# First expert block's rows gathered by column products from x1 in two tile pairs, with key products and slot table moved behind the first up products

## The reference, cut to what matters

```python
x = x + gt1 * rmsnorm(y, norm_gains[l, 1])
h = rmsnorm(x, norm_gains[l, 2]) * (1.0 + sc2) + sh2
...
group_sel = jnp.argmax(group_logits, axis=-1)
top_p, top_i = lax.top_k(jax.nn.softmax(in_group, axis=-1), TOP_K_IN_GROUP)
expert_ids = group_sel[:, None] * EXPERTS_PER_GROUP + top_i
...
for e in range(N_EXPERTS):
    hid = jax.nn.silu(t @ w_up1[e]) * (t @ w_up3[e])
    y = y + combine[:, e:e + 1] * (hid @ w_down[e])
```

## Time and profile before

| | |
|---|---|
| median of 3 runs | 1086.32 us (1085.09 to 1086.57) |
| profiled execution | 1088.07 us, its span 1086.4 us |
| PE busy | 1023.9 us (94%) |
| DVE busy | 657.9 us (61%) |
| ACT busy | 329.8 us (30%) |
| POOL busy | 135.3 us (12%) |
| moved by DMA | 275.10 MB, 253 GB/s mean |

### The profile page before, as it was taken

One profiled execution on the slowest core, in us unless ns is written; L12 is line 12 of the kernel. 1 busy time (PEld: TensorE's weight loads), 2 busy tenths in 40 slices (PEclk: granted clock), 3 DMA queues, 4 the chain that ended last, 5 costly groups with the idle time before them and its releaser, 6 DMA issues.

```text
span 1086.4 us, 18111 instructions
## 1 busy us (share of the span) xinstructions
PE 1023.9 (94%) x7385; PEld 588.7 (54%) x7385; DVE 657.9 (61%) x1125; ACT 329.8 (30%) x512; POOL 135.3 (12%) x156
## 2 busy tenths in 40 slices
PE   4899999999999999999999999999999999889995
PEld 2578578755556777768884444444433433333342
DVE  2478869364465442248347677777777666566666
ACT  3352462375662324364353110111111110110114
POOL 0100000200000101374401100000000000001003
PEclk9899999999999999999998999999999999999998
DMA  9666403204420004242747999999999999999994
GB/s 343 249 208 216 171 1 137 93 3 162 148 78 2 4 5 157 80 156 98 306 194 310 363 396 401 400 397 403 406 409 407 401 404 392 405 397 400 411 421 194
DMA packets 67733, 275.10 MB, mean 253 GB/s; under 512 B 7742, under 2 KB 17256, under 8 KB 43098
## 3 DMA queue, kind: packets, MB, share of 16 engines
q1 hardware_dynamic: 62976, 263.71, 62.7%
q10 hardware_dynamic: 2218, 6.52, 1.6%
q0 software_dynamic: 2480, 4.01, 1.3%
HBM read 274.13 MB, written 4.21 MB: 256 GB/s over the span
## 4 chain that ended last, share of the span: by engine, by line
PE 50%; SPq 23%; DVE 12%; DMA 7%; ACT 5%; issue 2%; POOL 0%; DVEq 0%; ACTq 0%
SPq L488 16%; PE ps L2231 9%; PE ps L2250 5%; SPq L492 5%; PE ps L1897 3%; DMA arena<-in_w_up 3%; PE ps L2214 2%; SPq L496 2%; PE ps L1878 2%; DMA arena<-in_w_mod 2%; PE ps L1886 2%; PE ps L1995 2%; PE ps L1844 2%; PE ps L1879 1%; PE ps L1880 1%
## 5 line engine op out<-in xcount | busy, mean ns | idle before, releaser
L1558 DVE TENSOR_TENSOR arena<-arena,ps 128x1024 f32<-128x1024 f32 x124 | 145.5, 1215 | 52.6 <-PE ps L2214 52.6
L2231 PE MATMUL ps<-arena 128*64 128x512 f32 x672 | 154.5, 602 | 11.1 <-DMA arena<-in_w_up 10.4
L2231 PEld LDWEIGHTS ps<-arena 128*64 128x64 f32 x672 | 47.8, 138 | 105.0 <-issue 101.3
L1062 ACT ACTIVATE results<-ps,ST 64x512 fp32r<-64x512 f32 x64 | 43.7, 683 | 182.7 <-PE ps L2250 182.2
L1055 ACT ACTIVATE arena<-ps 128x256 f32<-128x256 f32 x32 | 12.3, 384 | 233.9 <-PE ps L2231 233.9
L2250 PE MATMUL ps<-arena 128*64 128x512 f32 x336 | 76.7, 598 | 1.5 <-DMA arena<-in_w_down 1.5
L1735 PE MATMUL ps<-h_upper,w_upper 128*128 128x512 f32 (+1 forms) x184 | 73.9, 402 | 4.4 <-POOL h_lower_first L616 4.2
L2231 PE MATMUL ps<-ring,arena 128*64 128x512 f32 x320 | 72.7, 596 | 4.3 <-DMA ring<-in_w_up 4.3
L1568 DVE SCALAR_TENSOR_TENSOR results<-ps,ST,results 64x512 fp32r<-64x512 f32 x64 | 48.0, 750 | 46.8 <-ACT results L1062 46.3
L2214 PE MATMUL ps<-results,back 128*128 128x512 f32 x248 | 73.8, 419 | 0.0
L1737 PE MATMUL ps<-h_upper,w_lower 128*128 128x512 f32 (+1 forms) x184 | 72.5, 394 | 0.0
(11 more groups left out here) (440 smaller groups left out, 1835.1 us busy)
## 6 DMA issues: line engine op xcount, KB each, us to landing
arena<-in_w_up SPq DMA_DIRECT2D x84, 1024.0 KB, 28.0
ring<-in_w_up SPq DMA_DIRECT2D x44, 1024.0 KB, 27.3
ring<-in_w_down SPq DMA_DIRECT2D x11, 2048.0 KB, 32.3
arena<-in_w_down SPq DMA_DIRECT2D x11, 2048.0 KB, 30.1
arena<-in_w_down SPq DMA_DIRECT2D x20, 1024.0 KB, 27.3
ring<-in_w_mod SPq DMA_DIRECT2D x6, 2048.0 KB, 8.8
arena<-in_w_mod SPq DMA_DIRECT2D x6, 2048.0 KB, 9.4
ring<-in_w_in SPq DMA_DIRECT2D x6, 2048.0 KB, 8.3
```

The lines of the kernel that those rows point to most:

```text
L1558: TT(two_banks(acc[:, t, :]), two_banks(acc[:, t, :]), ps[:, BACK_BANK[t]:BACK_BANK[t] + 2, :], ALU.add).then_inc(back_added, 1)
L2231: last = mm(ps[64 * hf:64 * hf + 64, UP_BANK, :].rearrange("p (m n) -> p m n", m=2), turned_rows[:, k, :], up_pair(u, k)[:, :, 256 * hf:25 ...
```

## The change

On PE the first block's rows now come as columns: for each k, a product whose stationary operand is every eighth column of `x1` and whose moving operand is `picked` gives the turned rows at once (`first_rows_of`). It is done for pairs of k, and for tiles 0 and 1 before the last ranks, for tiles 2 and 3 between the first up products. ACT scales one k at a time, and the up products of the first block wait for one k at a time. The slot table moves between the up products of k = 5 and k = 6, with half its products. The key rows become 16 products of 128 columns in BF16 behind the up products, copied out by ACT. The slot weights, the rows of block 1 and DVE's weight factors move behind the first block's hidden values. One idle product is left of seven.

```diff
-            sp.wait_ge(rows_moved, 16 * 4 + 2)
...
-            A(hrow[0][:, 0:512], ps[0:CAP, 0, :], ACT.Copy).then_inc(rows_moved, 1)
-            A(hrow[0][:, 512:1024], ps[CAP:2 * CAP, 0, :], ACT.Copy).then_inc(rows_moved, 1)
...
+            nc.scalar.preload_act_table_set("silu_and_others")
+            act.wait_ge(rows_moved, 16 * 4)
             for k in range(KD):
-                last = A(hgT_first[:, k, :], ps[:, 0, CAP * k:CAP * k + CAP], ACT.Identity, scale=V("A1", k), bias=V("SH1", k))
-            last.then_inc(hg_ready, 1)
+                if k % 2 == 0:
+                    act.wait_ge(first_picked, k // 2 + 1)
+                A(hgT_first[:, k, :], ps[:, PICK_BANK[k // 2], CAP * (k % 2):CAP * (k % 2) + CAP], ACT.Identity, scale=V("A1", k), bias=V("SH1", k)).then_inc(part_ready, 1)
             act.wait_ge(route_ready, 1)
-            nc.scalar.preload_act_table_set("silu_and_others")
             again = act.value_load(nblk_i[0:1, 20:21], min_val=LOOPED // NSET - 1, max_val=(LOOPED + MAXO) // NSET - 1)
...
+                if first:
+                    act.wait_ge(table_done, 2)
+                    A(key_rows[:, :, :], ps[:, BACK_BANK[1]:BACK_BANK[1] + 2, :], ACT.Copy).then_inc(back_added, 1)
...
+            def pick_matrix(t0):
+
+                of = lambda a: a[:, t0:t0 + 2]
+                link(TT(o1(of(chose0)), of(oh)[:, :, 0:1], o1(V("rs", 8 + t0, 2)), ALU.mult))
+                dve.wait_ge(rank_done, t0 // 2 + 1)
...
+                TT(of(picked), of(picked), o1(of(chose0)).broadcast_to((P, 2, CAP)), ALU.mult).then_inc(pick_ready, 1)
+
+            pick_matrix(0)
             dve.wait_ge(rstd2, NT)
...
-            for c in range(2):
-                TT(key_diag[:, c], ident3.broadcast_to((P, NT, P)), o1(key[:, NT * c:NT * c + NT]).broadcast_to((P, NT, P)),
-                   ALU.mult).then_inc(factor_ready, 1)
...
+            TS(key_parts[:, 0, :], blk_, CAP / FAR, None, ALU.mult).then_inc(factor_ready, 1)
+            TS(key_parts[:, 1, :], rr, 1.0 / FAR, None, ALU.mult).then_inc(factor_ready, 1)
...
+            def first_expert_dve():
+
+                dve.wait_ge(sil_ready, 1)
+                TT(hid, sil, ps[:, UP_BANK, 256:512], ALU.mult).then_inc(hid_ready, 1)
+                slot_factors()
+                dve.wait_ge(ht_done, 1)
+                CP(hidT, ps[:, 1, 0:256]).then_inc(ht_ready, 1)
+                ohw = selw.rearrange("p c t b -> p (c t) b")
+                for i in range(N2):
+                    TS(ohw[:, i, :], K("iota64")[:, 0:MAXB], blk_[:, i:i + 1], routf[:, i:i + 1], ALU.is_equal, ALU.mult).then_inc(factor_ready, 1)
+                dve.wait_ge(back_added, 1)
+                back_rows(0, 0)
+                dve.wait_ge(table_done, 3)
+                CP(w_slot, ps[:, BACK_BANK[0], 0:MAXB]).then_inc(table_ready, 1)
+                dve.wait_ge(table_ready, 2)
+                rows_turned_in(2, by_part=True)
+                yo_lower(1, w_now[:, 0:1])
...
+            def first_rows_of(pair, t0):
+
+                for a in range(2):
+                    for t in (t0, t0 + 1):
+                        last = mm(ps[:, PICK_BANK[pair], CAP * a:CAP * a + CAP],
+                                  x1[:, t, :].rearrange("p (q k) -> p k q", k=KD)[:, 2 * pair + a, :], picked[:, t, :],
+                                  start=(a == 0 and t == 0), stop=(t == NT - 1), skip_group_check=True)
+                return last
+
+            router_logits(NT - 2)
+            ranks(0).then_inc(rank_done, 1)
+            transposes_x1(NT - 1)
+            router_logits(NT - 1)
+            pe.wait_ge(pick_ready, 1)
+            for pair in range(KD // 2):
+                first_rows_of(pair, 0)
+            idle_products(1)
             ranks(2).then_inc(rank_done, 1)
...
+            def first_up():
+
+                pe.wait_ge(pick_ready, 2)
+                first_rows_of(0, 2).then_inc(first_picked, 1)
+                for k in range(KD):
+                    if k % 2 == 0 and k < KD - 2:
+                        first_rows_of(k // 2 + 1, 2).then_inc(first_picked, 1)
+                    last = first_up_part(k)
+                    if k == KD // 2 - 1:
+                        last.then_inc(up_half, 1)
+                    if k == KD // 2:
+                        last.then_inc(hg_done, 1)
+                    if k == KD - 3:
+                        pe.wait_ge(part_ready, KD)
+                        slot_tokens()
+                last.then_inc(up_done, 1)
...
+            first_up()
+            slot_keys()
+            expert_down(0, 0, None)
+            slot_weights()
+            turn_rows(1, 1)
+            for u in range(1, NSET):
+                expert(u, 0, u, by_part=(u == 1))
```

More of the change, by code:

```diff
@@ L1066, in _ @@
             for u in range(NSET):
-                expert_act(u + 1, w_now[:, u:u + 1], NSET)
+                expert_act(u + 1, w_now[:, u:u + 1], NSET, first=(u == 0))
             with act.Fori(0, again) as it:
@@ L1584, in back_rows, with expert_dve @@
                     TS(slot_key, slot_key, float(NSET * CAP), None, ALU.add).then_inc(back_step, 1)
-            def expert_dve(before, rows, weight, first=False, last=False):
-                if not first:
-                    add_back(0, NT * before - 3)
-                    add_back(1, NT * before - 2)
+            def first_expert_dve():
[14 more added lines that the diff above has]
+                yo_lower(1, w_now[:, 0:1])
+            def expert_dve(before, rows, weight, last=False):
+                add_back(0, NT * before - 3)
+                add_back(1, NT * before - 2)
                 rows()
@@ L2174, in ranks @@
                 return last
-            ranks(0)
-            ranks(2).then_inc(rank_done, 1)
-            idle_products(1)
-            pe.wait_ge(pick_ready, 1)
-            for t in range(NT):
-                for h in range(2):
-                    last = mm(ps[CAP * h:CAP * h + CAP, 0, :], picked[:, t, :], x1[:, t, 512 * h:512 * h + 512], start=(t == 0), stop=(t == NT - 1))
-            last.then_inc(table_done, 1)
-            idle_products(1)
+            def first_rows_of(pair, t0):
[13 more added lines that the diff above has]
+            idle_products(1)
+            ranks(2).then_inc(rank_done, 1)
             def turned(u):
@@ L2215, in send_back, with first_up_part @@
                 return ins
-            def expert_up(u, it, before):
-                turned_rows = hgT_first if before is None else hgT
-                pe.wait_ge(hg_ready, NSET * it + (u + 1))
+            def first_up_part(k):
+                pe.wait_ge(part_ready, k + 1)
+                if k % (KD // 2) == 0:
+                    pe.wait_ge(w_in_sem[0][2 * k // KD], 32)
+                for hf in range(2):
+                    last = mm(ps[64 * hf:64 * hf + 64, UP_BANK, :].rearrange("p (m n) -> p m n", m=2), hgT_first[:, k, :],
+                              up_pair(0, k)[:, :, 256 * hf:256 * hf + 256], start=(k == 0), stop=(k == KD - 1))
+                return last
@@ L2263, in slot_weights, with expert @@
                 last.then_inc(table_done, 1)
-            for c in range(2):
-                pe.wait_ge(factor_ready, 2 * NT + 1 + c + 1)
-                last = mm(ps[:, BACK_BANK[1] + c, :], K("ones"), key_diag[:, c].rearrange("p t q -> p (t q)"), start=True, stop=True)
-            last.then_inc(table_done, 1)
-            def expert(u, turn, before, last=False):
-                expert_up(u, turn, before)
-                if before is None:
-                    slot_weights()
+            def expert(u, turn, before, last=False, by_part=False):
+                expert_up(u, turn, before, by_part)
                 if not last:
@@ L2277, in expert @@
                 expert_down(u, turn, before)
-            for u in range(NSET):
-                expert(u, 0, u if u else None)
+            first_up()
[3 more added lines that the diff above has]
+            turn_rows(1, 1)
+            for u in range(1, NSET):
+                expert(u, 0, u, by_part=(u == 1))
             pe.wait_ge(route_ready, 1)
```

145 lines of the change are left out of this document (72 added, 73 removed).

## The result

| | before | change |
|---|---|---|
| median | 1085.7 us (4 runs on that chip, 1084.67 to 1086.57) | 1095.1 us (4 runs, 1091.88 to 1095.87) |
| ratio | 1 | 1.0083, 95% interval 1.0064 to 1.0102 |
| profiled execution | 1088.07 us | 1095.7 us, its span 1093.8 us |
| PE busy | 1023.9 us | 1031.0 us |

The forecast was 1083.7 us in a range of 1077.0 to 1088.0, faster. The time lies 7 us above the range, on the side to which I had given 0.12.

A forecast was written before the change was run, and what follows sets the result against it. The weight stream bounds the kernel. Fourth issue 0.4 us earlier plus 4.0 of queue gives 4.4, less 1.75 for one half-clock stretch: 2.65 off the 1086.32 median, 1083.7 us, range 1077.0 to 1088.0.

The forecast's parts named there:

- the stream: Weight loads feeding the expert blocks; claimed to set the kernel's end and to start 4.4 us earlier.
- the fourth issue: SP's first load for block 1's buffer, before at 611.73; claimed to come at 611.3, early by 0.4 us.
- Up to `picked`: PE and DVE until the second half of `picked`; claimed ready at 585.1, 2.7 us later than before, at half clock.
- From there to the fourth issue, at full clock: PE from `picked` to SP's load for block 1's buffer; claimed +26.0 us, and 0.2 to the issue.
- `up_half` at +6.8: Three column-product pairs at 1.09 us each and half the up products (7.09 / 2), counted from `picked`.
- The fourth pair: 1.09: Last pair of column products for tiles 2 and 3, between the first up products; claimed to take 1.09 us.
- The down products start at +16.3: First block's down products, counted from `picked`; slot table ends at +10.6, then 5.7 us for SiLU, product, copy, factors.
- +26.0: End of the PE sum from `picked`: down products 3.65, slot weights, turned rows, scaled k, half of block 1's up products.
- Rival 3: Column products' strided weight loads cost half as much again, 5.7 us on the path: slower, 1089.4 us; chance 0.12.
- Rival 1: PE's clock stays up through the column products: gain 8.7 us, 1077.6 us; chance 0.20.
- Rival 2: Both low-clock stretches come, the second under the first up products: gain 0.9 us, 1085.4 us; chance 0.28.
- The queue's slack: Queueing of the first piece for block 1's buffer, 4.0 of its 9.2 us; claimed as added gain.

The follow-up runs named there:

- contiguous: The change with column products reading 128 neighbouring columns of `x1` instead of every eighth one: 1088.40 us, 1.0025 of the kernel before.
- rows_back: The change with row products of 512 columns, copied and turned, plus four idle products, in place of column products: 1084.49 us, 0.9978 of the kernel before.
- zeros_later: The change with POOL's two memsets waiting until DVE has copied the first block's hidden values: 1090.46 us, 1.0033 of the kernel before.
- parts: The change with column pairs read at step 8 over 64 and 32 partitions, then steps 3 and 8 over 128: 1095.34 us, one run.
- rows_no_idle: As rows_back, without the four idle products ahead of the last ranks: 1088.38 us, 1.0016 of the kernel before.
- factors_late: The change with DVE's slot factors behind the copy of the hidden values, POOL's memsets left in place: 1090.76 us, 1.0039 of the kernel before.
- idle_each: The change with an idle product behind each of four column-product pairs of tiles 0 and 1, four for one: 1097.74 us, 1.0087 of the kernel before.
- rows_best: As rows_back, with POOL's memsets behind the hidden values' copy and ACT's block-count load behind the first three blocks: 1082.63 us, 0.9966 of the kernel before.

## Why the prediction was wrong

The frame was right: the stream decides, the fourth issue decides the stream, and where it comes decides the time. The sum up to that issue was wrong, 611.3 against 622.09. Step by step:

- **Up to `picked`.** Foreseen 585.1, measured 584.03 + 0.29 = 584.32. This held, in part by luck, as errors of both signs nearly cancel: the clock fell only at 576.5, so the router's products ended 1.9 us earlier (572.79 against 574.7); the 32 column loads took 580.46 - 572.79 = 7.67 us against 7.0, and `picked` came 2.05 behind the start of the ranks, not 1.55. That the last ranks wait for PE and not for DVE was right: DVE sat idle for 4.5 us.
- **"From there to the fourth issue, at full clock": three pairs and half the up products, `up_half` at +6.8.** It came near 597.4, at +13.1. This is the step that failed most: the price of a pair, taken from the turned rows, and the clock, taken as full. The three pairs took 4.00 + 2.11 = 6.1 us against 3.27 (2.8 more), by the price of the strided loads; the two groups of up products took 3.61 + 3.29 = 6.9 against 3.55 (3.35 more), by the half clock that I had taken to be over. *contiguous* takes back about half of each (4.64 and 5.17 us, its first two pairs and first up products still at half clock); *rows_back* has no such pairs, and its up products ran at full clock.
- **"The fourth pair: 1.09."** 2.05 us, so 1 us more, from the same price.
- **"The down products start at +16.3"**, 5.7 behind the slot table: 7.9 measured. ACT's wait for the block count is in it as foreseen (SiLU 1.1 us behind the end of the up products, foreseen 1.2). The memsets of POOL, which the prediction did not name, are 2.85 us of it: in *zeros_later* PE waited 0.77 us in place of 3.62. The rest was taken a little too long; the weight factors, read as 1.1 us, are 0.9 in the trace of before. The memsets stood in that trace too, at 595.9 to 599.6, and moved with the slot table by 10 us, onto DVE's copies. This is a collision between two engines by a third thing that they share; I had looked at semaphores and queues only.
- **"+26.0."** From the start of the down products 12.0 us against 9.9: the clock fell once more, as foreseen, and at 5.45 us in place of 3.65 for the down products it cost the 1.75 that I had given it. I had taken it off the result and not put it into this sum, and had allowed for no other; with the long one ahead of it there were two.

The pieces make 2.8 + 3.35 + 1.0 + 2.2 + 2.1 = 11.45 us, less the 0.8 by which `picked` was early: 10.65 of the 622.09 - 611.3 = 10.8 us.

**The rivals.** Rival 3 named the right mechanism. It asked for half as much again per load; the price is 0.13 us above what I had taken at full clock (0.14), and 0.02 at half. So its sign, loads over 0.26 apart at half clock, did not show (0.24): the price lay at the level where I had not put a sign. I had held against it that the turned rows pay nothing for their step. That was the wrong row: it has the step and the columns, but it is a transpose, and *parts* shows that an FP32 product pays whatever the partitions. Rival 3's own price, 5.7 us, would have given 1089.4 us; the loads cost 0.7 + 2.8 + 1.0 = 4.5 us, and the rest is the clock and the memsets. That it was given only 0.12 was the fault of that row. Rival 1 is out, the clock did not stay up. Rival 2 had the second fall in the right place but priced it at 1.75 us where it was one long stretch of 20.5 us.

**The queue's slack**, taken as 4.0 us, came out as 10.36 - 7.6 = 2.8 in the two profiled executions. The first piece did land 5.2 us behind its issue in place of 9.2, as the 4.0 had it; where the stream lost the rest was not followed.

**What the change gained.** *rows_back* has everything of the change but the column products, and it is faster than the kernel before by 0.22% (0.10 to 0.34). So the slot table, the key products and the slot weights behind the first up products, and the earlier choice, are worth that much, even with POOL's collision in it; but only with the idle products back, since *rows_no_idle* is slower by 0.16% (0.03 to 0.29). The column products, with the idle products that they displaced, cost the change 1095.1 - 1084.49 = 10.6 us, across two chips; by the ratios to the kernel before it is 1.05%, or 11.4 us.

## What to carry to other kernels

Price an operation by a row that agrees with it in kind, operand layout and type, and where none does, keep the far bound in the sum: here the stationary operand's step, from four FP32 elements on, doubled the price of a load at full clock (0.24 us in place of 0.11) and added little at half (0.24 against 0.22). When work moves in time, look not only at what waits for it but at what it newly lies beside: the memsets kept nobody on the path waiting in one place and cost 3 us in another, by holding up DVE's copies within SBUF. And PE fell to half clock here amid small and strided products in a row, with no gap above 0.18 us, and the dense up products behind them paid for it (3.6 us for eight in place of 1.9), so idle products in a wait (*rows_back* against *rows_no_idle*, 4 us) are taken out only when the granted clock of that stretch has been looked at.

## What was not expected of the hardware

- A weight load of 128 FP32 columns for a product costs 0.11 to 0.12 us at steps of 1 and 2 elements at full clock (0.22 at half) and 0.24 at steps of 4 and 8, at full and at half clock nearly alike, and, at half clock, from 32, 64 and 128 partitions nearly alike.
- DVE's copy of three elements within SBUF took 3.38 us beside POOL's memsets, a copy of 256 elements a partition out of PSUM 0.42, a product of two tensors within SBUF 0.16.
- The same instructions lose the clock at different moments: counted from the start of the last router products, 5.5 us in the change, 4.2 in *factors_late* and 2.9 in *idle_each*, which are alike on PE up to there. Half clock then lasted 20.5 us in the change and in *zeros_later* and 17.1 in *factors_late*. What sets the moment was not found.
- An indirect fetch of 64 rows, which landed 3.9 to 4.1 us after its issue before, took 9.3 to 9.5 in the change and 9.7 to 10.5 in *rows_best*, when megabytes of weights had been issued just ahead of it.
